# Two transformer blocks on one core: weight splits and half of a gain product move from VectorE to GpSimd at three block boundaries

## The reference

```
h = h + rms_norm(mix, norm_mix_post)            # end of the mixer
ffn = swiglu_ffn(rms_norm(h, norm_ffn_pre), w_gate_up, w_down)
h = h + rms_norm(ffn, norm_ffn_post)            # end of the block
```

## Time and profile before

| | |
|---|---|
| runs | 995.86, 999.44, 997.89 us (median 997.89) |
| the profiled execution | 995.86 us, its span 994.1 us, granted TensorE clock 0.992 |
| TensorE matmuls busy | 948.6 us (95%) |
| VectorE busy | 669.4 us (67%) |
| ScalarE busy | 544.3 us (55%) |
| GpSimd busy | 260.9 us (26%) |
| chain that ended last | PE 81%, ACT 6%, DVE 6%, DMA 3% |

### The profile page before, as it was taken

The page is one execution under the profiler, slowest core; times in us unless marked ns, Lnnn a source line. Parts: engine busy times, 40 slices in busy tenths (PEclk is TensorE's granted clock), DMA queues, the critical chain, the costliest instruction groups (busy, mean ns, idle before and its releaser), DMA issues.

```text
span 994.1 us, 16477 instructions
## 1 busy us (share of the span) xinstructions
PE 948.6 (95%) x6119; PEld 832.5 (84%) x6119; DVE 669.4 (67%) x1082; ACT 544.3 (55%) x956; POOL 260.9 (26%) x245
## 2 busy tenths in 40 slices
PE   7999999999989999889999999989989999999997
PEld 6987777888877798889989999988889878888786
DVE  4766667777787668955666666676966677755553
ACT  5567566444434558634446466556854564444443
POOL 4304102111123154679931043330230021000010
PEclk9999999999999999999999999999999999999999
DMA  8755347788888715560128556652226767665662
GB/s 260 227 168 168 111 149 237 230 286 280 276 297 289 232 44 144 153 169 23 29 94 272 179 165 179 174 142 84 77 94 210 248 206 224 218 207 170 195 216 77
DMA packets 141466, 179.02 MB, mean 180 GB/s; under 512 B 8010, under 2 KB 117260, under 8 KB 141392
## 3 DMA queue, kind: packets, MB, share of 16 engines
q1 hardware_dynamic: 130624, 144.53, 47.0%
q0 software_dynamic: 10176, 33.16, 11.0%
q10 hardware_dynamic: 592, 0.34, 0.1%
HBM read 176.89 MB, written 1.12 MB: 179 GB/s over the span
## 4 chain that ended last, share of the span: by engine, by line
PE 81%; ACT 6%; DVE 6%; DMA 3%; issue 2%; POOL 1%; ACTq 0%; DVEq 0%; SPq 0%
PE bank L1912 27%; PE bank L2001 12%; PE bank L2003 12%; PE bank L2002 12%; PE bank L2170 1%; ACT w_hi L857 1%; DVE w_lo L1318 1%; DVE isc L1716 1%; PE bank L2429 1%; PE bank L1943 1%; PE bank L2425 1%; PE bank L2449 1%; PE bank L2364 1%; PE bank L2536 1%; PE bank L2053 1%
## 5 line engine op out<-in xcount | busy, mean ns | idle before, releaser
L1318 DVE TENSOR_TENSOR w_lo<-w_raw,w_hi 128x1024 fp32r<-128x1024 f32 (+1 forms) x227 | 274.2, 1234 | 91.4 <-ACT w_hi L857 85.0
L857 ACT ACTIVATE w_hi<-w_raw 128x1024 fp32r<-128x1024 f32 (+1 forms) x258 | 262.0, 1037 | 127.9 <-PE bank L2003 49.7
L1912 PE MATMUL bank<-h_hi,w_hi 128*128 128x256 f32 x560 | 165.1, 295 | 6.2 <-POOL w_lo L706 2.1
L1912 PE MATMUL bank<-h_lo,w_hi 128*128 128x256 f32 x560 | 159.8, 285 | 0.0
L1912 PE MATMUL bank<-h_hi,w_lo 128*128 128x256 f32 x560 | 159.6, 285 | 0.0
L2001 PE MATMUL bank<-w_hi,h_hi 128*128 128x512 f32 x384 | 151.7, 395 | 1.9 <-DVE h_lo L1318 1.9
L2003 PE MATMUL bank<-w_hi,h_lo 128*128 128x512 f32 x384 | 149.8, 390 | 0.0
L2002 PE MATMUL bank<-w_lo,h_hi 128*128 128x512 f32 x384 | 149.5, 389 | 0.0
L706 POOL TENSOR_TENSOR w_lo<-w_raw,w_hi 128x1024 fp32r<-128x1024 f32 (+1 forms) x39 | 86.0, 2205 | 151.1 <-DVE w_lo L1318 112.4
L1912 PEld LDWEIGHTS bank<-h_hi,w_hi 128*128 128x128 f32 x560 | 108.6, 194 | 7.8 <-POOL w_lo L706 2.3
L1912 PEld LDWEIGHTS bank<-h_lo,w_hi 128*128 128x128 f32 x560 | 108.8, 194 | 0.0
(11 more groups left out here) (458 smaller groups left out, 1821.3 us busy)
## 6 DMA issues: line engine op xcount, KB each, us to landing
w_raw<-in_w_in SPq DMA_DIRECT2D x84, 512.0 KB, 3.8
ada_raw<-in_ada_w POOLq DMA_DIRECT2D x48, 512.0 KB, 6.2
w_raw<-in_w_gate_up SPq DMA_DIRECT2D x88, 256.0 KB, 5.4
w_raw<-in_w_ffn_in SPq DMA_DIRECT2D x88, 256.0 KB, 3.9
w_raw<-in_w_down SPq DMA_DIRECT2D x22, 512.0 KB, 7.3
w_raw<-in_w_ffn_out SPq DMA_DIRECT2D x22, 512.0 KB, 4.6
w_raw<-in_w_out SPq DMA_DIRECT2D x16, 512.0 KB, 4.4
w_raw<-in_w_o_ssd SPq DMA_DIRECT2D x16, 512.0 KB, 3.4
```

The lines of the kernel that those rows point to most:

```text
L857: act.activation(high(u, n), w_raw[:, u % RING, 0:n], ACT.Copy).then_inc(hi_ready, 1)
L1318: return dve.tensor_tensor(dst, src, hi.bitcast(F32), ALU.subtract)
L1912: ins = pe.matmul(out_b[:, s, :], w[:, kk, c], x[:, k0 + k, :], start=k == 0 and s == 0 and step == 0, stop=k == sum(st.ks) - 1 and s == 1 ...
```

## The change

`pool_lows` now holds all four held units, so GpSimd makes all twelve low parts of the three boundaries. GpSimd also takes the first 512 columns of `gain_x` for each t, and its order at each boundary is written out. VectorE keeps the other 512 columns. On VectorE `piece_lo` 3 of t = 0 moves behind the two `new_x` of t = 1. On ScalarE the high part of `v+3` moves ahead of `piece_hi` 0 and 1 of t = 0, and `square_m1`/`root_m` of t = 1 move behind these two.

```diff
-    pool_held = tuple(st.u0 + 3 for st in NEXT)
-    pool_lows = frozenset(u for part in (pool_held, pool_u, pool_lat, pool_topk, pool_conv) for u in part)
+    pool_lows = frozenset(u for part in (held, pool_u, pool_lat, pool_topk, pool_conv) for u in part)
@@ GpSimd
+        def gain_x(b, t):
+            pool.wait_ge(pre_in, 16 * (b + 1))
+            pool.wait_ge(x_new, 4 * b + 2 * t + 1)
+            pool.tensor_tensor(m_tok[:, t, 0:512], x_tok[:, t, 0:512], pre_rows[b][:, 0:512], ALU.mult
+                               ).then_inc(xg_ready, 1)
+
+        def boundary(b):
+            v = NEXT[b].u0
+            split(v)
+            split(v + 1)
+            gain_x(b, 0)
+            split(v + 2)
+            split(v + 3)
+            gain_x(b, 1)
...
-        split(pool_held[0])
+        boundary(0)
...
-        split(pool_held[1])
+        boundary(1)
...
-        split(pool_held[2])
+        boundary(2)
@@ ScalarE, boundary
             split_to(v + 3)
             square_x(b, 0)
+            split_to(v + 4)
+            piece_hi(b, 0, 0, bias)
+            piece_hi(b, 0, 1, bias)
             square_m1(b, 1)
             root_m(b, 1)
-            piece_hi(b, 0, 0, bias)
-            piece_hi(b, 0, 1, bias)
-            split_to(v + 4)
             piece_hi(b, 0, 2, bias)
@@ VectorE
         def gain_x(b, t):
-            for c in range(2):
-                half = slice(512 * c, 512 * c + 512)
-                dve.wait_ge(x_new, 4 * b + 2 * t + c + 1)
-                ins = dve.tensor_tensor(m_tok[:, t, half], x_tok[:, t, half], pre_rows[b][:, half], ALU.mult)
-            ins.then_inc(xg_ready, 1)
+            dve.wait_ge(x_new, 4 * b + 2 * t + 2)
+            dve.tensor_tensor(m_tok[:, t, 512:1024], x_tok[:, t, 512:1024], pre_rows[b][:, 512:1024], ALU.mult)
@@ VectorE, boundary
-            v = NEXT[b].u0
-            split_to(v + 2)
+            split_to(NEXT[b].u0 + 4)
             gained(b, 1, 0)
...
             rstd_x(b + 1, 0)
-            split_to(v + 4)
             piece_lo(b, 0, 0, bias)
             piece_lo(b, 0, 1, bias)
             gained(b, 1, 1)
             piece_lo(b, 0, 2, bias)
             rstd_m(b, 1)
-            piece_lo(b, 0, 3, bias)
             new_x(b, 1, 0)
             new_x(b, 1, 1)
+            piece_lo(b, 0, 3, bias)
             gain_x(b, 1)
```

## The result

The changed kernel took **1009.76 us** (median of 4 runs, 1007.31 to 1011.36), the kernel before 996.88 in the same comparison: ratio 1.0118, 95% interval 1.0086 to 1.0151. Two later comparisons on other executions gave 1.0093 (1.0062 to 1.0123) and 1.0070 (1.0050 to 1.0090). The kernel is slower, as forecast, and by more than forecast: the forecast was 1003.8, the range ended at 1006.5.

A forecast was written before the change was run, and what follows sets the result against it. TensorE, 81% of the chain, was taken as the bound. Boundary terms 1.9 + 2.5 + 1.5 = +5.9 us on the profiled 995.86 gave 1001.8; adding 2.03 gave 1003.8, own range 1001.5 to 1006.5, 8-in-10 range 997 to 1006.5.

The forecast's parts named there:

- What bounds, and where: TensorE is 81% of the chain; time moves only where it waits at the three boundaries, 4.5 us at most to gain.
- `new_x` behind the split of `v+1`: At t = 0 of boundaries 0, 1, 2, `new_x` stands until GpSimd's split ends: +0.95, +0.23, +0.49 us.
- The half gain: After the second `new_x`, GpSimd's `gain_x` half takes 1.6 to 1.7 us; VectorE's half follows, about 0.5 more.
- `diag` stands behind the split of `v+2`: At t = 0 `diag` waits out GpSimd's split; first turns at boundaries 0, 1, 2 move +2.95, +1.68, +2.5 us.
- Rival A: `diag` of t = 0 isn't blocked; `new_x` and the gain alone delay first turns: +0.6 us, 998.5, chance 0.22.
- B: VectorE's `new_x` and `diag` win against GpSimd at both t: -1.5 us, 996.4, or -4.5, 993.4; chance 0.11.
- C: `diag` and the t = 1 `new_x` both stand behind GpSimd at each boundary: +9 us, 1007, chance 0.07.
- What is given back at t = 1: At boundaries 0 and 2 the second `diag` hides behind t = 0 matmuls, leaving second turns +1.9 and +1.5 us.
- `piece_lo` 3 at boundary 1: At boundary 1 the last low piece, now behind two `new_x`, comes late for TensorE's short steps: +2.5 us.
- From one execution to the median: For the whole kernel, the median was taken to stand 2.03 us above the profiled execution: 1001.8 becomes 1003.8.

The follow-up runs named there:

- the filled kernel: The changed kernel with 15 and 17 identity products on TensorE ahead of its wait for the first turn at boundaries 0 and 2; 1004.15 us, ratio 1.0066.

## Why the prediction was wrong

- **What bounds, and where.** Right: all of the cost that repeats lies at the three boundaries.
- **`new_x` behind the split of `v+1`.** Right: +1.01, +0.34, +0.57 where +0.95, +0.23, +0.49 were forecast. The run with GpSimd waiting for `diag` shows it alone: first turns +1.07, +0.27, +0.56.
- **The half gain.** Right in order and length (1.64 to 1.67; forecast 1.6 to 1.7).
- **`diag` stands behind the split of `v+2`.** Right, and it decides the first turns: +2.95, +1.78, +2.62 for 2.95, 1.68, 2.5 (at boundary 2 the closeness is in part luck, as said under the table). Rival A is dead by the 2.18 in the rows above; B too; of C nothing is seen, no second turn waits. The rule of the Trainium skill weighed there ("SBUF — State Buffer", section "Who interferes with whom") is borne out for this operation: a tensor_scalar of 128x128 took 2.18 behind a split and 0.29 without it.
- **What is given back at t = 1: the step that failed**, in its sizes: boundary 0 at +1.9 and boundary 2 at +1.5. I let the products of t = 0 run at their old speed from a turn 2.5 to 3 us late (`152.65 + 7.3`). They didn't: after 3.66 and 4.10 us of idle time TensorE ran at 1.2 GHz for a stretch. Measured +3.52 and +2.92, that is 1.62 and 1.43 more. With the idle time filled the two terms are 1.90 and 1.49, and from turn to turn it takes 7.32 and 7.69 where I had 7.3 and 7.7, so the arithmetic of the step was right and a term was missing, the clock behind the idle time, which I had put at nothing without a word: **+3.1 us** in all, which puts the sum at 5.9 + 3.1 = 9.0 for the 9.2 measured.
- **`piece_lo` 3 at boundary 1.** +2.78 for 2.5: 0.93 is the order by itself, and nearly all the rest the first turn that comes 1.78 later.
- **From one execution to the median.** I added 2.03 us for both kernels alike. In the first comparison the median stood 1.02 above the profiled execution for the kernel before and 5.82 for the changed one. So the 12.9 us are 9.2 at the boundaries, -1.1 elsewhere in the profiled pair, and 4.8 here. The first comparison met more low clocks in the changed kernel (0.985) than the later ones did (0.988, 0.989), and their medians, 1005.24 and 1006.15, lie inside my range with the same term missing: there the number would have held by luck.
- **What stays open.** Whether the change makes low clocks likelier outside the boundaries is not shown. At equal clock 6.4 us remain, near the 6.2 that the filled kernel shows at the boundaries; but the slope puts the whole of the lower clock at 1.8 us where the traces of the boundaries have 3.1, and the filled kernel's mean lies 6.9 above that of before. The slope is a correlation over executions, and the two prices were not brought together.

The missing term could be read in the kernel before. Its own timeline has an idle time of 2.05 us and then, by windows, a granted clock of 0.65 with TensorE fully busy; another of 2.93 us ends at 666.80, and from 668.25 the clock is down (0.57). The 0.65 at 441 follows idle times of 1.02 and 1.70 us that end at 437.26 and 440.22.

```profile
411.45 0.39 PE L1912 MATMUL bank<-h_hi,w_hi 128*128 128x256 f32 x1 [2.05 <-POOL w_lo L706]
```

```profile
413.00:417.00 4.00, 4.00 (x26) 4.00 (x25) 3.72 (x13) 0.00 (x0) 3.71 (x3) 0.65 0.79 246
441.00:444.00 3.00, 3.00 (x16) 2.72 (x15) 2.05 (x4) 0.00 (x0) 1.36 (x2) 0.65 0.82 222
668.00:672.00 4.00, 4.00 (x21) 3.52 (x20) 2.16 (x3) 2.30 (x7) 0.00 (x0) 0.57 0.27 56
```

I had forecast idle times of 3 to 4 us in so many words and looked up nothing for what follows such a time. The Trainium skill says so too ("TensorE: Matmul & The Clock Gate", section "Why this matters for your kernels"): it advises against idle gaps between bursts of matmuls, since the clock drops behind them. The trace agrees, with the 0.57 behind 3.66 us.

## What to carry to other kernels

A wait that leaves the bounding engine idle is paid twice if its clock falls behind it: when a forecast puts TensorE to sleep for some microseconds, look in the same trace for other idle times of that length, read the granted clock behind them, and add what the slow stretch cost (here 1.3 to 2.1 us each). GpSimd's long elementwise work belongs where VectorE has none of the operations on the path that stand behind it (here `new_x`, `gain_x` and `diag`): with the two engines it is the order of asking that counts, and an unrelated split ahead of a 0.29 us operation costs its whole remainder. Order each boundary by what its next products read first; the same order of pieces gained about 1 us from turn to turn where the steps are long and lost 0.9 where they are short.

## What the runs showed of the hardware

- Behind idle times of 3.48 to 4.64 us before a first turn at boundaries 0 and 2, TensorE ran at the lower level each time (ten turns in five profiles). Behind 2.54 and 2.56 us it did once and once not; behind 0.71 to 2.04 us before these turns never, but behind 2.05 us at 411.45 of the kernel before it did, and in the changed kernel's profile the same matmuls, behind 2.06 us at 421.09, ran at 1.00 (421 to 425.5). The length of the idle time before is not enough to tell; the price when it comes is 1.3 to 2.1 us from turn to turn.
- GpSimd can get in between two VectorE instructions of the same kind issued back to back: two `new_x` that take 1.41 took 4.54 with a third split between them, and the three splits ran 7.72 us without a gap.
- Not every VectorE operation stands behind GpSimd. In the changed kernel `gained`, which reads the product in PSUM and one row in SBUF, took 0.69 at 148.48, inside GpSimd's splits (145.55 to 150.48), and 0.68 at 144.59 ahead of them; `new_x`, issued at 149.28 with two SBUF tensors, stood.
